# Cached keys of a decoder step's samples: turned by transposing DMAs and merged by GpSimd, in place of turned by TensorE

## The reference, cut to what matters

```python
def dilated_branch_sample(q, kc, vc, dil):
    T = q.shape[1]
    wb = kc.shape[1] - T
    j = jnp.arange(KEYS_PER_BRANCH + 1)
    idx = wb + jnp.arange(T)[:, None] - dil * j[None, :]
    valid = idx >= 0
    idxc = jnp.maximum(idx, 0)
    kg = kc[:, idxc]
    vg = vc[:, idxc]
    s = jnp.einsum("bthd,btjhd->bthj", q, kg).astype(jnp.float32) * (HEAD_DIM ** -0.5)
    s = jnp.where(valid[None, :, None, None], s, -jnp.inf)
    m = jnp.max(s, axis=-1, keepdims=True)
    p = jnp.exp(s - m)
    den = jnp.sum(p, axis=-1, keepdims=True)
    o = jnp.einsum("bthj,btjhd->bthd", (p / den).astype(vc.dtype), vg)
```

## Time and profile before

| | us |
|---|---|
| median of 3 runs | 1763.01 (1760.7 to 1763.08) |
| span of the profiled execution | 1761.8 |
| TensorE busy | 1712.2 |
| VectorE busy | 1127.0 |
| ScalarE busy | 876.3 |
| GpSimd busy | 2.2 |

### The profile page before, as it was taken

How to read it: one execution, slowest core, us unless ns; L and a number is a source line. 1 busy time by engine, 2 the same in 40 slices (tenths; PEclk the granted TensorE clock), 3 DMA queues, 4 the chain that set the end, 5 groups by cost and what they waited for, 6 DMA issues and landing times.

```text
span 1761.8 us, 30467 instructions
## 1 busy us (share of the span) xinstructions
PE 1712.2 (97%) x12158; PEld 1595.8 (91%) x12158; DVE 1127.0 (64%) x2077; ACT 876.3 (50%) x1645; POOL 2.2 (0%) x12
## 2 busy tenths in 40 slices
PE   7999999999999999999998999999999999999998
PEld 7999999756668999888778899999999999999998
DVE  5499998686675677345467667644576533676633
ACT  7322223655667676555455455534545533555433
POOL 0000000000000000000000000000000000000000
PEclk9999999999999999999999999999999999999999
DMA  8233221365315645443533334444445444444443
GB/s 247 64 119 114 84 86 37 132 225 192 127 43 154 185 144 156 149 131 108 164 120 96 118 114 140 133 136 138 133 143 155 139 140 139 132 144 147 144 136 100
DMA packets 349219, 233.74 MB, mean 133 GB/s; under 512 B 7979, under 2 KB 322465, under 8 KB 349071
## 3 DMA queue, kind: packets, MB, share of 16 engines
q1 hardware_dynamic: 344232, 222.96, 41.4%
q10 hardware_dynamic: 4847, 8.83, 1.4%
HBM read 220.68 MB, written 11.50 MB: 132 GB/s over the span
## 4 chain that ended last, share of the span: by engine, by line
PE 85%; DVE 7%; ACT 4%; issue 3%; SPq 1%; DMA 0%; ACTq 0%; DVEq 0%
PE bank L1240 79%; PE bank L1237 6%; ACT whi L621 1%; SPq L458 1%; DVE cv L1841 1%; DVE wlo L1854 1%; DMA raw<-in_w_mk_dram 0%; DVE Y L1841 0%; DVE Pp L1845 0%; DVE RSCF L1977 0%; DVE Pp L2130 0%; ACT wide L635 0%; DVE op_lo L1841 0%; DVE XT L2232 0%; DVE C L1981 0%
## 5 line engine op out<-in xcount | busy, mean ns | idle before, releaser
L1240 PE MATMUL bank<-op_hi,whi 128*128 128x352 f32 x1632 | 539.5, 331 | 4.9 <-DVE wlo L1854 2.6
L1854 DVE TENSOR_TENSOR wlo<-raw,whi 128x1024 fp32r<-128x1024 f32 (+1 forms) x312 | 373.8, 1200 | 246.0 <-ACT whi L621 245.7
L1240 PE MATMUL bank<-op_hi,wlo 128*128 128x352 f32 x1632 | 525.4, 322 | 0.0
L1240 PE MATMUL bank<-op_lo,whi 128*128 128x352 f32 x1632 | 524.5, 321 | 0.0
L621 ACT ACTIVATE whi<-raw 128x1024 fp32r<-128x1024 f32 (+1 forms) x312 | 325.1, 1043 | 287.7 <-PE bank L1240 94.5
L1240 PEld LDWEIGHTS bank<-op_hi,whi 128*128 128x128 f32 x1632 | 307.5, 188 | 14.6 <-issue 9.9
L1240 PEld LDWEIGHTS bank<-op_lo,whi 128*128 128x128 f32 x1632 | 308.4, 189 | 0.6
L1240 PEld LDWEIGHTS bank<-op_hi,wlo 128*128 128x128 f32 x1632 | 307.3, 188 | 0.0
L1240 PE MATMUL bank<-fhi,whi 128*128 128x352 f32 x528 | 171.2, 324 | 0.0
L1240 PE MATMUL bank<-fhi,wlo 128*128 128x352 f32 x528 | 170.7, 323 | 0.0
L1240 PE MATMUL bank<-h1hi,whi 128*128 128x352 f32 x480 | 158.0, 329 | 0.0
(11 more groups left out here) (287 smaller groups left out, 2299.7 us busy)
## 6 DMA issues: line engine op xcount, KB each, us to landing
raw<-in_w_up_dram SPq DMA_DIRECT2D x132, 512.0 KB, 3.7
raw<-in_w_down_dram SPq DMA_DIRECT2D x48, 512.0 KB, 3.7
raw<-in_w_out_dram SPq DMA_DIRECT2D x24, 512.0 KB, 3.8
raw<-in_w_xq_dram SPq DMA_DIRECT2D x24, 512.0 KB, 3.8
raw<-in_w_xo_dram SPq DMA_DIRECT2D x24, 512.0 KB, 3.8
raw<-in_w_in_dram SPq DMA_DIRECT2D x20, 512.0 KB, 3.8
raw<-in_w_down_dram SPq DMA_DIRECT2D x24, 384.0 KB, 3.3
cached<-in_cache_win_k_dram SPq DMA_DIRECT2D x8, 1024.0 KB, 5.9
```

What stands on the lines that cost most here:

```text
L1240: return pe.matmul(out, lhsT, rhs, start=first, stop=last, skip_group_check=shared)
L1854: dve.tensor_tensor(wlo[v % SLOTS][:, 0:nk, :], raw[v % SLOTS][:, 0:nk, :], whi[v % SLOTS][:, 0:nk, :].bitcast(F32), ALU.subtract).then_in ...
```

## The change

Keys no longer go through TensorE's transposes. The fp32 rows are looked at as pairs of 16-bit halves. For each sample, on the SP queue:
- `turn_near` turns the 512 near rows by one transposing DMA into `KT2n` (128 x 8 x 512 of 16 bits), `turn_old` the 384 far rows by four into `KT2o`. After it, even partitions hold low halves, odd ones high halves.
- `part_near` and `part_old` copy that, by four DMAs each from SBUF to SBUF, into `KPn` and `KPo`: low and high halves in one partition each, side by side.
- GpSimd's `merge_keys` interleaves the halves into the fp32 tile `KM` (128 x 4 x 896), two copies for the near and two for the far part.
- TensorE's `key_scores` makes four products of 512 columns (slot 7i+3) and four of 384 (slot 7i+6) for sample i of a group.

`KT2n`, `KPn` and `KT2o` lie in ring slots 0 to 2, so the three w_out weights come only after the last sample's keys. `KPo` lies where the value buffer `cached1` is. There are two value buffers; windows of values have seven DMAs (the far rows are now in another order, as the bias table is). The prompt's value products always use PSUM bank 4; before it was bank 3 where key transposes used bank 4.

```diff
-    cached = [mn(f"cached{i}", o, [P, KTILES, AW]) for i, o in enumerate((160064, 47104, 119808))]
+    cached = [mn(f"cached{i}", o, [P, KTILES, AW]) for i, o in enumerate((119808, 47104))]
+    KM = mn("KM", 160064, [P, AT, KEYS])
+    KT2n = place("KT2n", RING, [P, 2 * AT, NEAR], U16)
+    KPn = place("KPn", RING + 8192, [P, AT, 2, NEAR], U16)
+    KT2o = place("KT2o", RING + 16384, [P, 2 * AT, OLD], U16)
+    KPo = mn("KPo", 47104, [P, AT, 2, OLD], U16)
...
+    KEY_SLOTS = {KTILES * i + (3 if part == "near" else 6): (part, i) for i in range(4) for part in ("near", "old")}
...
+        def turn_near(b):
+            if b:
+                sp.wait_ge(*at("kpn", (b - 1, 1, 1)))
+            rows = A["cache_win_k"][0, b].rearrange("s h d -> s (h d)").bitcast(U16)
+            sp.dma_start_transpose(KT2n[:, :, :], rows[WB - NEAR:WB, :]).then_inc(*mark("ktn", b, 16))
...
+            for r in range(4):
+                sp.dma_start_transpose(KT2o[:, :, r * OLDR:(r + 1) * OLDR], rows[0:OLDR, r, :]).then_inc(*mark("kto", (b, r), 16))
...
+        def part_near(b):
+            sp.wait_ge(*at("ktn", b))
+            if b:
+                sp.wait_ge(*at("km", (b - 1, "near", 1)))
+            for e in range(2):
+                for h in range(2):
+                    sp.dma_start(KPn[DH * e:DH * e + DH, :, h, :], KT2n[h:P:2, e:2 * AT:2, :]).then_inc(*mark("kpn", (b, e, h), 16))
...
+        sp.wait_ge(*at("unit", LAST_IN - 3))
+        turn_near(0)
+        sp.wait_ge(*at("unit", LAST_IN - 2))
+        part_near(0)
+        sp.wait_ge(*at("unit", LAST_IN - 1))
+        turn_old(0)
         sp.wait_ge(*at("unit", LAST_IN))
-        window(1)
+        turn_near(1)
+        part_old(0)
+        turn_old(1)
+        part_near(1)
+        turn_near(2)
         sp.wait_ge(*at("csq_used", 2 * CH - 1))
         sp.wait_ge(*at("cn", (CONV_ORDER[CH - 1], CT - 1)))
-        window(2)
...
+        window(0)
+        part_old(1)
+        turn_old(2)
+        for b in range(2, BD):
+            part_near(b)
+            if b + 1 < BD:
+                turn_near(b + 1)
+            if b == 4:
+                sp.wait_ge(*at("km", (3, "old", 1)))
+                window(1)
+                for i in range(2, 5):
+                    sp.wait_ge(*at("spv", i - 2))
+                    window(i)
+                sp.wait_ge(*at("spv", 3))
+            part_old(b)
+            if b + 1 < BD:
+                turn_old(b + 1)
+            if b == 2:
...
+        def merge_keys(b, part, src, c0, c1):
+            if b:
+                pool.wait_ge(*at("ssc", (b - 1, part)))
+            halves = KM[:, :, c0:c1].bitcast(U16).rearrange("p k (n h) -> p k h n", h=2)
+            for h in range(2):
+                pool.tensor_copy(halves[:, :, h, :], src[:, :, h, :]).then_inc(*mark("km", (b, part, h)))
...
+        def key_scores(part, b):
+            g, i = divmod(b, 4)
+            c0, c1, bk = (0, NEAR, 6) if part == "near" else (NEAR, KEYS, 7)
+            pe.wait_ge(*at("km", (b, part, 1)))
             for k in range(AT):
-                ins = turn(bank[4 + n % 2][:, k * P:(k + 1) * P], cached[c][:, a, k * P:(k + 1) * P])
-            ins.then_inc(*mark("ktr", n))
...
+                ins = mm(bank[bk][32 * k:32 * k + 32, 0:c1 - c0], QW[:, g, P * i + 32 * k:P * i + 32 * k + 32], KM[:, k, c0:c1], i == 0 and bk == 6, i == 3, True)
+            ins.then_inc(*mark("ssc", (b, part)))
```

More of the change, by code:

```diff
@@ L337, in layout @@
     SAMPLE = 44
-    ORDER_W = [(kind, b) for g in range(2) for kind in "kv" for b in range(4 * g, 4 * g + 4)]
+    OLD_PIECES = []
+    for r in range(4):
+        g = 0
+        while g < OLDR:
+            a, p = divmod(NEAR + r * OLDR + g, P)
+            n = min(P - p, OLDR - g)
+            OLD_PIECES.append((r, g, n, a, p))
+            g += n
     EARLY = 14
@@ L470, in load_x, with window @@
                 load(xt[i][0:NS, :], A["x_sample"].rearrange("b t d -> (b t) d"), f"x_in{i // 4}", i)
[L472 to L479, removed]
+        def window(b):
+            rows = A["cache_win_v"][0, b].rearrange("s h d -> s (h d)")
+            dst, name = cached[b % 2], f"cached{b % 2}"
+            load(dst[:, 0:NEAR // P, :], rows[WB - NEAR:WB, :].rearrange("(a p) n -> p a n", p=P), name, (b, "near"))
+            for j, (r, g, n, a, p) in enumerate(OLD_PIECES):
+                load(dst[p:p + n, a, :], rows.rearrange("(g r) n -> g r n", r=16)[g:g + n, r, :], name, (b, j))
@@ L488, in _ @@
             weight(g + 1)
-        for u in range(SLOTS, XFIRST + SLOTS - 1):
+        for u in range(SLOTS, XFIRST):
             weight(u)
@@ L527, in _ @@
+        for u in range(SLOTS - 1):
+            if u == 0:
+                sp.wait_ge(*at("kpn", (BD - 1, 1, 1)))
+            if u == 1:
+                sp.wait_ge(*at("km", (BD - 1, "near", 1)))
+            if u == 2:
+                sp.wait_ge(*at("kpo", (BD - 1, 1, 1)))
+            weight(XFIRST + u)
+        sp.wait_ge(*at("km", (BD - 1, "old", 1)))
+        window(5)
+        for b in range(6, BD):
+            sp.wait_ge(*at("spv", b - 2))
+            window(b)
         for e in range(2):
@@ L608, in _ @@
         pool.memset(QO[:, :, :, :], 0.0).then_inc(*mark("qzw0", 1))
+        for b in range(BD):
+            if b:
+                pool.wait_ge(*at("kpn", (b, 1, 1)))
+                merge_keys(b, "near", KPn, 0, NEAR)
+            pool.wait_ge(*at("kpo", (b, 1, 1)))
+            merge_keys(b, "old", KPo, NEAR, KEYS)
     @block.scalar
@@ L1417, in product @@
             i, hp = STEPS[s]
-            take(product_bank(s), "att", s)
+            take(4, "att", s)
             for e in range(2):
```

86 lines of the change are left out of this document (37 added, 49 removed).

## The result

The changed kernel takes 1884.99 us (median of 4 runs, 1884.41 to 1886.86) against 1763.05 before on the same chip: a ratio of 1.0695, interval 1.0679 to 1.071. It is slower, as forecast, but by 122 us and not by 26; the time lies outside the range of 1751 to 1850.

What follows compares the result with a forecast made beforehand. It took TensorE, busy 97%, as the bound, with late keys through the SP queue costing more than TensorE saves. Terms 30.5 + 3.5 + 2 - 10 = +26 on a span of 1761.8 gave 1789 us; range 1751 to 1850.

Steps and rivals of the forecast that it cites:

- term one: First group: keys late through the SP queue, far 3 merged at 409.5, slot 27 due at 379.0; +30.5 us.
- The rival that the supply keeps up: Key supply, both groups: keys arrive in time, term one only +1, no second-group stall; 1751.5 us, chance 0.17.
- term one's price of the copies: SP queue's key line: transfers at 0.35 MB/us, 2.0 us for a landing, 0.4 us for an issue.
- my rival of half rate: Transposing loads on the key line run at half a plain load's rate: +58 us, 1821; chance 0.25.
- quarter-rate figure of 1885: Same slow-loads rival: transposing loads at a quarter of the plain rate give about 1885 us.
- What would show it: Signs in the profile after: KM waits some 30 us, slot 27 about 409, outputs about 381, steps 14 to 24 about 62.
- Term two: Value windows, two buffers instead of three: 0.5 us for window 2 and 3 for window 3; +3.5 us.
- Term three: TensorE's clock after the last stall, near 409: half of 6 us at low clock lost; +2 us.
- Term four: Second group of four samples: gain 16, stall 6.0 waiting for far 7 at slot 71; -10 us.
- gain of 16: Second group: TensorE saves 19 us, less 3 for waits on VectorE; 5.06 us a step instead of 6.5.
- lower bound: Key line's fastest case: seven lines take 41.8 us from 335, 3.2 more for merges at 0.93 ns; 380.0.

Runs made afterwards that it cites:

- same_stride: Changed kernel with the four copies of each part writing every second partition instead of 64 adjoining ones, queries not rearranged (wrong rows, same cost): 1827.7 us (1.0366).
- second_group_half: second_group_2 with GpSimd's merging copies of the low halves left out for samples 5 to 7: 1761.3 us (0.9993).
- second_group_2: Kernel before with the change for samples 4 to 7 only, same-step copies, far keys in the loads' order, windows in seven pieces: 1773.2 us (1.0057).
- order_full_2: Complete changed kernel with same-step copies, queries rearranged, late first merge, reordered SP queue, outputs, value windows 2 and 3 and second-group queries moved: 1794.6 us (1.0186).
- group_2_late_turns: second_group_2 with near 4's and far 4's transposing loads issued one and two value windows later: 1773.1 us (1.005).

## Why the prediction was right and where it was wrong

- **The mechanism of term one was right.** The supply of keys through SP's queue is the bound of the first group, and its seven long stalls, 77 us in all, are waits for `KM`. The rival that the supply keeps up is out. The size was wrong: term one, 30.5 us, measures 77.3 (slot 27 at 456.3 against 379.0).
- **The step that failed is term one's price of the copies**: "I price transfers at 0.35 MB/us", taken from loads and used for copies from SBUF to SBUF. The four near copies take 10.15 us for 1 MB, 0.103 MB/us with their landing, where 5.0 were priced; the far ones 7.65, where 4.2 were. The mixed pairing of partitions makes it (4.75 and 4.31 with every second partition on both sides), and `same_stride` gives 57 us of the 122 back. An estimate from the queue's rows: of the 12.6 us a sample over the price (28.0 against 15.4), the copies are 9.9 (10.5 + 8.6 against 5.0 + 4.2) and the loads 2.7 (8.9 of issues against 6.2).
- **The issue of a transposing load**, 0.4 and 4 x 0.6 us, measures 3.6 to 4.4 and 4 x 1.3. Its data come at nearly a plain load's rate (6.2 against 5.3 us with issue and landing), against my rival of half rate; the Trainium skill, Advanced Engine Details and Errata, section X-Bar Transpose (TRN2), says so, and the runs agree. That rival's quarter-rate figure of 1885 is met by the number alone; loads at a quarter of the rate don't occur.
- **What would show it**: the waits for `KM` up to slot 27 are 77 us and not some 30, the longest, 17.7, ahead of near 3 as foretold; the merges of 2.45 and 1.88 us lie in or just under the 2.1 to 2.9 foretold, and the low clock came; but outputs start at 422 and not at 381, slot 27 at 456 and not at 409, steps 14 to 24 take 97.6 us and not 62.
- **Term one had no start delay.** Sample 0's near merge at 319 stopped VectorE and cost 6.3 us. I gave the merge's length (1.4 ns an element, measured 1.2; 4.8 and 3.7 us a pair) but not what it does to VectorE.
- **Term two**, 3.5 us, is 19.5, and mostly not by the windows it named. The product of window 1 waits 9.9 us and that of window 3 waits 5.5; window 2's doesn't wait. Window 1, priced at nothing, has the memory of `KPo`: it may be loaded only after far 3's merge, at 456.3, and in the queue it stands behind near 4's copies and near 5's turn, so that its load is issued from 472.2 on. The rest is for the most part low clock: the products of windows 1 and 3 take 3.21 us where those of 0 and 2 take 1.74.
- **Term three**, 2 us, was sized for one stall. With twelve waits for `KM` the granted clock is 0.56 from 345 to 453 and 0.77 from 510 to 600. How much of the 122 is clock alone no run isolates.
- **Term four**, -10, is +26. Its stall, 6.0, is 27.0, in five waits for `KM`: the same slow supply. Of its gain of 16 some 1 us is left (27.0 against 25.9), with the clock at 0.77. And even with keys in time these 16 us hang on VectorE being free: `second_group_half` shows 7.6 us gained in steps 14 to 25, `second_group_2` 6.5 lost, and between them stands only GpSimd's merging. "VectorE ... has 42.9 of work" left out GpSimd's 35 us of merging, which hold up part of that work.
- By the prediction's own price of 0.93 ns, the two copies of its lower bound take 2.9 us and not 3.2; nothing hangs on that.
- What stays open: why the copies are slower from every second partition to adjoining ones than the other way, and what causes the remaining 31 us of `order_full_2`; its trace only places them, 12.4 ahead of slot 27, 12.2 at the value windows and 6.5 in the second group.

## What to carry to other kernels

Work taken off a bound engine is worth only what its replacement's slowest link allows: count the replacement's pass time per item (every issue, landing and reuse of a buffer in one queue) and hold it against the item's time on the engine, here 28 us a sample against 10.9 in the first group and 17.9 in the second (a fourth of 43.7 and of 71.7). Price a copy by its partitions on both sides, not by its bytes alone; here every second partition on both sides, or all 128, was fastest. And count an idle GpSimd as free only where VectorE is idle too, or runs nothing of the kind that stopped here.

## What the hardware showed that I had not expected

- Copies of 1 MB in SBUF: 4.75 us between every second partition, 6.4 from 64 adjoining ones to every second, 6.9 and 7.2 with adjoining ones on both sides, 10.15 from every second to adjoining ones.
- Issuing a transposing load occupies the SP queue by itself: mostly 3.6 to 4.4 us for 512 rows of 2 KB, 1.2 to 1.3 for 96, and for the 512 under load 10.0 (`second_group_2`) and 14.0 (`group_2_late_turns`), both at a DMA share of 1.14.
- GpSimd's copies exclude VectorE's instructions with two operands in SBUF, in either direction (1.83 us of products took 6.39, and a copy of 2.45 took 17.8), and stop its scalings too (0.88 took 9.55); a reciprocal of 1.25 and the maxima from PSUM of 0.69 took no longer beside a copy.
- GpSimd's copy of 1536 elements takes 1.9 us where it writes every second 16-bit place, and 7.0 to 7.7 where it writes every eighth.
